# Attention of a two-model layer stack: heads in pairs on the two halves of TensorE's array, forget decays added by a selecting product

## What is computed

```
def causal_block_attention(q, k, v, log_forget_cum=None):
    s = einsum('bqhd,bkhd->bhqk', q_i, k) * dk ** -0.5
    if has_decay:
        s = s + d_queries[..., :, None] - d_keys[:, :, None, :]
    s = where(key_pos <= q_pos, s, -inf)
    p = softmax(s, axis=-1)
    return einsum('bhqk,bkhd->bqhd', p, v)

fox = causal_block_attention(fq, fk, fv, cumsum(log_sigmoid(f_logit + b_f), axis=1))
mla = causal_block_attention(q, k, v)
return concatenate([rms(fox), rms(mla)], -1) @ w_o
```

## Time and profile before

| | us |
|---|---|
| median of 3 runs | 2843.33 |
| lowest and highest of them | 2840.07, 2846.72 |
| the profiled execution | 2859.1 |
| its span | 2857.3 |
| TensorE busy | 2260.7 (79%) |
| VectorE busy | 687.8 (24%) |
| ScalarE busy | 372.7 (13%) |

### The profile page before, as it was taken

The page is one execution under the profiler, slowest core; times in us unless marked ns, Lnnn a source line. Parts: engine busy times, 40 slices in busy tenths (PEclk is TensorE's granted clock), DMA queues, the critical chain, the costliest instruction groups (busy, mean ns, idle before and its releaser), DMA issues. The chain is left out here.

```text
span 2857.3 us, 31837 instructions
## 1 busy us (share of the span) xinstructions
PE 2260.7 (79%) x13320; PEld 1411.6 (49%) x13321; DVE 687.8 (24%) x1524; ACT 372.7 (13%) x741; POOL 25.7 (1%) x28
## 2 busy tenths in 40 slices
PE   7897778899677996899866666689788998666765
PEld 5564436565244855778622222267576885222322
DVE  4352104352012135346300000012443112000001
ACT  1331001331001003110200000010312011000000
POOL 0000000000000000000000000000000000000000
PEclk9799899799898998889978888899988998878888
DMA  9138999135997340058499999964200345999997
GB/s 391 79 118 345 428 429 397 62 118 237 429 428 328 147 161 0 1 227 340 156 428 428 428 429 428 427 270 175 88 1 1 118 176 231 428 428 428 429 428 317
DMA packets 55834, 779.42 MB, mean 273 GB/s; under 512 B 6840, under 2 KB 7096, under 8 KB 8120
## 3 DMA queue, kind: packets, MB, share of 16 engines
q1 hardware_dynamic: 55736, 778.02, 65.5%
HBM read 776.95 MB, written 1.05 MB: 272 GB/s over the span
## 5 line engine op out<-in xcount | busy, mean ns | idle before, releaser
L1715 PE MATMUL bank<-ring,arena 128*32 128x512 f32 x3136 | 499.5, 773 | 337.7 <-DMA ring<-in_w_exp 334.2
L1715 PEld LDWEIGHTS bank<-ring,arena 128*32 128x32 f32 x3136 | 101.4, 126 | 728.4 <-DMA ring<-in_w_exp 494.3
L1740 PE MATMUL bank<-ring,arena 128*32 128x512 f32 x1568 | 197.4, 643 | 70.7 <-DMA ring<-in_w_exp 47.9
L853 PE MATMUL bank<-xnT,ring 128*128 128x256 f32 x960 | 212.7, 385 | 9.5 <-ACT xnT L368 9.5
L1895 DVE TENSOR_TENSOR arena<-bank,arena 128x256 f32<-128x256 f32 (+1 forms) x33 | 18.3, 554 | 787.6 <-PE bank L1715 559.3
L853 PEld LDWEIGHTS bank<-xnT,ring 128*128 128x128 f32 x960 | 185.6, 194 | 37.2 <-issue 11.2
L1446 PE MATMUL bank<-xnT,ring 128*128 128x256 f32 x768 | 178.5, 387 | 10.6 <-PEq L981 10.6
L1446 PEld LDWEIGHTS bank<-xnT,ring 128*128 128x128 f32 x768 | 149.1, 194 | 33.3 <-issue 12.2
L1685 PE MATMUL bank<-arena 128*128 128x256 f32 x592 | 141.5, 393 | 3.6 <-DVE arena L1906 3.6
L1685 PEld LDWEIGHTS bank<-arena 128*128 128x128 f32 x592 | 112.4, 195 | 62.8 <-issue 48.5
L1740 PEld LDWEIGHTS bank<-ring,arena 128*32 128x32 f32 x1568 | 50.7, 113 | 186.1 <-issue 95.6
(11 more groups left out here) (332 smaller groups left out, 2352.2 us busy)
## 6 DMA issues: line engine op xcount, KB each, us to landing
ring<-in_w_exp SPq DMA_DIRECT2D x288, 2048.0 KB, 25.7
arena<-in_w_ada SPq DMA_DIRECT2D x24, 2048.0 KB, 11.9
ring<-in_w_in SPq DMA_DIRECT2D x20, 2048.0 KB, 20.6
ring<-in_w_merge SPq DMA_DIRECT2D x18, 2048.0 KB, 8.5
ring<-in_w_o SPq DMA_DIRECT2D x8, 2048.0 KB, 11.2
ring<-in_w_conv SPq DMA_DIRECT2D x6, 2048.0 KB, 27.3
ring<-in_w_rest SPq DMA_DIRECT2D x2, 1696.0 KB, 25.7
small<-in_small SPq DMA_DIRECT2D x2, 1440.0 KB
```

The source lines that it names most:

```text
L853: last = nc.tensor.matmul(o[:, T * j:T * j + T], w[:, k, col:col + P], xnT[:, k, :], start=k == 0, stop=k == KT - 1)
L1715: last = nc.tensor.matmul(o[rows(e), :], Xw[:, k, rows(e)], ring[:, slot(n), at:at + MW], start=k == 0, stop=k == KT - 1)
L1740: last = nc.tensor.matmul(o[rows(e), :], hidT[:, j, rows(e)], ring[:, slot(n), at:at + MW], start=j == 0, stop=j == ft - 1)
```

## The change

The table of constants gets four columns `pair` in place of four columns `chunk`. Column j of `pair` is 1 on the partitions whose number within its half of 64 is j.

The heads are taken in the order 8 to 15, then 0 to 7, in eight pairs. Scores, transposes and value products are listed pair by pair (scores(i), turn(i-2), product(i-3) for pair i). Within a fox pair, the even head's products (partitions 0 to 63, one bank) and the odd head's (partitions 64 to 127, another bank) alternate; within every pair the two heads' value products alternate too.

The decays are formed once per layer. VectorE writes the scaled logs into a zeroed matrix `lfx` (two small operations), TensorE multiplies it with the triangle (two products), ScalarE copies the result to `decay` (128x256): the decays of the even fox heads on partitions 0 to 3, those of the odd on 64 to 67. A score bank gets its decay by a product of `pick` (64 rows that are zero except for one row of ones) with one half of `decay`, over 128 and 256 columns. GpSimd clears `lfx` and builds `pick`. Six buffers `zb` and four `pT` replace three and two. The scaling of the probabilities stays on VectorE, and so do the masks, the maxima, the reciprocals and the copies into `mixT`.

```
+    put("pair", p[:, None] % HD == np.arange(HEADS // 2)[None, :])
...
+            order = list(range(HEADS, NH)) + list(range(HEADS))
+            zb = [ar(3072 + 384 * i, COLS) for i in range(6)]
+            pT = [ar(5456 + 384 * i, COLS) for i in range(4)]
...
+                    def scores(i):
+                        if i >= 2:
+                            pe.wait_ge(z_ready, 2 * i - 2)
+                        pair = (2 * i, 2 * i + 1)
+                        if order[2 * i] >= HEADS:
...
+                            return
+                        pe.wait_ge(decay_ready, 1)
+                        pe.wait_ge(pick_ready, 1)
                         for t, (a, b) in enumerate(parts):
+                            for n in pair:
+                                h = order[n]
+                                nc.tensor.matmul(score_bank[n % 4][:, a:b], fqT[part(h), h // 2, P * t:P * t + P], fkT[part(h), h // 2, 0:b - a],
+                                                 start=t == 0, stop=False, skip_group_check=True)
+                        for t, (a, b) in enumerate(parts):
+                            for n in pair:
+                                h = order[n]
+                                last = nc.tensor.matmul(score_bank[n % 4][:, a:b], pick[part(h), h // 2, :], decay[part(h), 0:b - a],
+                                                        start=False, stop=t == 1, skip_group_check=True)
...
+                    def decays():
+                        pe.wait_ge(decay_in, 2)
+                        nc.tensor.matmul(bank[5][:, 0:T], lfx[:, 0, :], K("tri")[:, 0:T], start=True, stop=False)
+                        nc.tensor.matmul(bank[5][:, P:T], lfx[:, 1, :], K("tri")[:, T + P:2 * T], start=False, stop=True).then_inc(decay_made, 1)
...
+                    def turn(i):
+                        for n in (2 * i, 2 * i + 1):
+                            pe.wait_ge(p_ready, 2 * n + 2)
+                            if n >= 2:
+                                pe.wait_ge(pT_ready, n - 1)
...
+                    def product(i):
+                        pe.wait_ge(pT_ready, 2 * i + 2)
...
+                        for t in range(TT):
+                            for n in (2 * i, 2 * i + 1):
...
+                @block.gpsimd
+                def _(pool):
+                    nc.gpsimd.memset(lfx, 0.0).then_inc(decay_in, 1)
+                    nc.gpsimd.tensor_tensor(pick, K("ones").unsqueeze(1).broadcast_to([P, HEADS // 2, P]), K("pair").unsqueeze(2).broadcast_to([P, HEADS // 2, P]),
+                                            ALU.mult).then_inc(pick_ready, 1)
...
-                    def decays(h):
-                        if h >= 2:
-                            dve.wait_ge(scores_ready, h - 1)
                         for s in range(TT):
-                            last = nc.vector.tensor_scalar(Z[h % 2][:, s, :], K("tri")[:, T * s:T * s + T], lf[:, s, h:h + 1], -1.0 / scale[0],
-                                                           ALU.mult, ALU.mult)
+                            last = nc.vector.tensor_scalar(lfx[:, s, :].rearrange("p (o r) -> p o r", o=2)[:, :, 0:HEADS // 2], lf[:, s, :].rearrange("p (j o) -> p o j", o=2),
+                                                           -1.0 / scale[0], None, ALU.mult)
...
+                    for n in range(NH + 6):
+                        if n < NH:
+                            softmax(n)
+                        if n == 0:
+                            decays()
+                        if 1 <= n <= NH:
+                            finish(n - 1)
+                        if n % 2 == 1 and n >= 7:
+                            take((n - 7) // 2)
...
+                    nc.scalar.preload_act_table(ACT.Exp)
+                    for n in range(NH + 3):
+                        if n < NH:
+                            exps(n)
+                        if n == 1:
+                            act.wait_ge(decay_made, 1)
+                            nc.scalar.copy(decay, bank[5][:, 0:T]).then_inc(decay_ready, 1)
+                        if n >= 3:
+                            to_sbuf(n - 3)
```

More of the change, by code:

```diff
@@ L572, in attention @@
             NH = 2 * HEADS
+            NPAIR = NH // 2
             COLS = P + T
[L574 to L579, removed]
+            decay_in, decay_made, decay_ready, pick_ready, scores_ready, z_ready, top_ready, e_ready, r_ready, p_ready, p_turned, pT_ready, out_ready, out_taken = (
+                sem(f"att_{n}") for n in ("decayin", "decaymade", "decay", "pick", "scores", "z", "top", "e", "r", "p", "turned", "pT", "out", "taken"))
+            order = list(range(HEADS, NH)) + list(range(HEADS))
+            zb = [ar(3072 + 384 * i, COLS) for i in range(6)]
+            pT = [ar(5456 + 384 * i, COLS) for i in range(4)]
+            pick = ar(7000, HEADS // 2, P)
+            lfx = ar(7512, TT, P)
+            decay = ar(7768, T)
             score_bank = [bank[i] for i in (0, 1, 6, 7)]
@@ L614, in turn @@
-                    def turn(h):
-                        pe.wait_ge(p_ready, 2 * h + 2)
-                        if h >= 2:
[L617 to L628, removed]
@@ new lines, in decays @@
+                    def decays():
[7 more added lines that the diff above has]
+                                pe.wait_ge(pT_ready, n - 1)
+                            for k in range(3):
+                                last = nc.tensor.transpose(bank[2 + n % 2][:, P * k:P * k + P], zb[n % 6][:, P * k:P * k + P], K("ident"))
+                            last.then_inc(p_turned, 1)
@@ L672, in _, with softmax @@
-                    decays(0)
-                    decays(1)
-                    for i in range(NH + 3):
-                        if i < NH:
-                            softmax(i)
-                        if 1 <= i <= NH:
-                            finish(i - 1)
-                        if i + 2 < HEADS:
-                            decays(i + 2)
-                        if i >= 4 and i % 2 == 0:
-                            take((i - 4) // 2)
+                    def softmax(n):
+                        z = zb[n % 6]
+                        dve.wait_ge(scores_ready, n + 1)
+                        if n >= 6:
+                            dve.wait_ge(p_turned, n - 5)
+                        nc.vector.scalar_tensor_tensor(z, score_bank[n % 4][:, 0:COLS], scale[order[n] // HEADS], K("causal"), ALU.mult, ALU.add).then_inc(z_ready, 1)
+                        dve.wait_ge(z_ready, n + 1)
+                        for t, (a, b) in enumerate(parts):
+                            last = nc.vector.tensor_reduce(top[n % 2][:, t:t + 1], z[:, a:b], AX, ALU.max, negate=True)
+                        last.then_inc(top_ready, 1)
```

101 lines of the change are left out of this document (45 added, 56 removed).

## The result

| | before | after |
|---|---|---|
| median of 4 runs, us | 2845.02 | 2807.42 |
| lowest and highest | 2840.07, 2847.91 | 2802.06, 2810.78 |
| the profiled execution (span) | 2859.1 (2857.3) | 2802.06 (2800.1) |
| first attention stage | 60.2 | 35.4 |
| second attention stage | 57.1 | 34.8 |

The ratio is 0.9868, 95% interval [0.9846, 0.989]: 37.6 us faster, between 31 and 44. The forecast was a gain of 46.1 and 2797, with a range of 2785 to 2822. The time lies in the range. The two profiles differ by 57.0 us and the two medians by 37.6, and most of this document is about that difference. One of the 19 further timings of the old kernel that stand beside the first experiments, 3005.8 us at a granted clock of 0.784, was in a slower state and is in none of the ratios.

What follows compares the result with a forecast made beforehand. It took TensorE to bound the old fox heads and VectorE the mla heads; with VectorE setting the pace, stages of 35.6 us instead of 60.2 and 57.1 gain 46.1, so 2843.3 - 46.1 = 2797 us, range 2785 to 2822.

Steps and rivals of the forecast that it cites:

- What bounds the new stage: Attention at the full clock: VectorE sets the pace in all 16 heads, 3.94 us a pair against TensorE's 3.6.
- TensorE's terms: Fox pair on TensorE: scores with decays 1.8 us, transposes 2 x 0.47, value products 0.9, together 3.6 us.
- The price of 0.229 us: Fox scores and decays: a 256-column product from 64 rows costs 0.229 us, because the array's halves work at the same time.
- The opening and the decays formed once: Stage start: first masking at 0.1 + 0.96 us; two small VectorE operations 0.3 us, counted as nothing, bound 0.5 a layer.
- The sum of a stage: One attention layer: first masking, 15 steps of 1.77 us, five copies of 0.40, then 6.0 to the end: 35.6 us.
- The gain: Both attention stages: 24.6 and 21.5 us off the profiled 60.2 and 57.1, together 46.1, taken from the median 2843.3.
- unchanged in length: Sign of being right: outside attention, the rest of the program keeps its length.
- I take it that the level stays: TensorE's clock in attention stays at the full level, since mla scores begin right behind the barrier; forecast chance 0.63.
- The lower level at the opening: First rival: the clock falls as before, mla heads run slow, costing 11.8 and 9.2 us; 2818 us, chance 0.18.
- the second: Rival: TensorE's halves don't overlap; 5.5 us a fox pair, 4.3 an mla pair, 8 us a layer; 2813, chance 0.10.
- the third: Rival: each product waits for an empty array, clock low throughout; stage 85 us, 53 us slower, 2896; chance 0.03.
- `head_rms_out` gave nothing back: Sign of being wrong: this block now begins at the lower level and gives 2 to 3 us back a layer.

Runs made afterwards that it cites:

- new_with_Z4: New kernel with decays added the old way (two VectorE operations and three full products a fox head), in four buffers written four heads ahead; 2817.6 us, stages 39.5 and 38.0.
- new_again: The new kernel unchanged, for a second profile and more times; median 2809.57 us, ratio 0.9879 to the kernel before; stages 33.8 and 34.7 us.
- old_third: The kernel before, unchanged, for a third profile; 2842.05 us, stages 46.3 and 54.1 us.
- new_norm_pool: New kernel with the two scalings of the probabilities per head moved from VectorE to GpSimd; one execution, 2794.5 us, both stages 30.2 us.
- new_norm_pool_timed: The new kernel with the scalings on GpSimd, run again for timing; median 2803.2 us, ratio 0.9851 to the kernel before.
- new_held: New kernel with TensorE held back at the attention's opening by nine VectorE mask copies whose results are unused; 2823.6 us, stages 40.5 and 40.1.
- new_all_in_turn: New kernel with each pair's two heads one after the other in scores, decays and values, instead of alternating; 2821.3 us, stages 45.8 and 36.9.

## Why the prediction was right, and where it was off

**What bounds the new stage: right.** VectorE sets the pace at 1.77 and 2.10 us (forecast 1.77 and 2.17). Two runs confirm it by taking work away (copies to ScalarE, scalings to GpSimd) and one by adding some (new_with_Z4).

**TensorE's terms: right, somewhat high.** Fox scores of a pair took 1.51 us for 1.8, value products 0.80 for 0.9, transposes 0.81 for 0.94, together 3.12 for 3.6. The price of 0.229 us from the pattern of the earlier trace rows held. The full-overlap end was the true one for the value products.

**The opening and the decays formed once: right.** The first masking starts 0.97 us after the stage opens (forecast 1.06), both small operations take 0.23 us (0.3). GpSimd builds `pick` in 1.04 us (0.5 to 1.9), unseen on the path.

**The sum of a stage: right as a total.** The last masking starts 131.38 - 103.06 = 28.3 us in, not 29.6: four copies lie ahead of it, not five, and the first step is 1.27 us long because there is nothing to scale yet. The end takes 138.50 - 131.38 = 7.1 us, not 6.0, half of it at the lower level, and 6.5 in the second layer. The errors cancel: the stages are 35.4 and 34.8 us for 35.6.

**The gain: the term that was mis-sized.** The step was "60.2 - 35.6 = 24.6 and 57.1 - 35.6 = 21.5", carried over to the median. It holds between the two profiles (24.8 and 22.3). But 30.7 + 23.9 us at the lower level were far more than the 0 + 17.1 of later executions. Two more profiles of the same program, with totals at the median, have stages of 46.3 and 54.1 us: against new_again's 33.8 and 34.7 this is a gain of 31.9, not 46.1. The prediction saw the 15.8 us between profile and median, allowed "up to a few microseconds" for them, and counted none. As far as these profiles tell it was all of it: 117.3 - 100.4 = 16.9 us.

With the line above, the gain of 47.1 between the profiles splits. At the full level throughout, the old stages are 2 x 46.3 = 92.6 us. So 117.3 - 92.6 = 24.7 was the old kernel's time at the lower level, and 92.6 - 70.2 = 22.4 is what the new stages, with the low stretches that they have, gain on an old one without any. In old_third against new_again it is 7.8 and 92.6 - 68.5 = 24.1. That part is the fox heads': one took 3.44 us at the full level and takes 3.87 / 2 = 1.94 now, and 8 x 1.50 = 12.0 us a stage is 24 in both. The mla heads' step on VectorE is 1.77 us without a copy in both kernels. Inside the fox heads the decays have a price of their own (new_with_Z4); the larger number of buffers was never changed by itself, so what it gives is not shown.

**What made up for it.** 31.9 us in the stages is less than the 37.6 of the medians. In the profile pair old_third and new_again, 36.0 us apart in total, the second model's block gives 25.4 - 18.7 = 6.7 more. It was at 1.00 in both profiles of the new kernel and at 0.66 in all three of the old one, with equal work. The prediction had the rest of the program "unchanged in length". Whether the new kernel brings this about by shifting what follows in time, or whether five profiles fell so by chance, I didn't test; variants with other stage lengths had 22.3 to 27.5 us there. The code alone doesn't decide it: new_norm_pool and new_norm_pool_timed are one kernel, and that block took 25.4 and 27.5 us in their first layers and 19.4 and 25.1 in their second. That part of the measured gain is observed and not explained.

**"I take it that the level stays": half right.** It stayed at the opening in both profiles of the new kernel, and fell later once or twice for 3.4 us. It cost little because TensorE has 0.75 us of slack in a pair and is off the path. Where it falls matters: new_again has one low stretch of 3.4 us in each layer, in the middle of the first stage (from 117.8 us) and at the end of the second (from 541.0 us), where TensorE is on the path, and the second stage is 0.9 us longer. Through the one in the middle VectorE's maskings keep their distances (117.59, 119.36 and 121.46 us: 1.77 and 2.10).

**The rivals.** The lower level at the opening came in new_held as that rival had it, behind an idle TensorE, but at 1 to 2 us a layer and not 9 to 12. The halves do overlap, even when not alternated (new_all_in_turn), so the second and the third had no ground; the third's 3.3 us a head on TensorE was 1.56. `head_rms_out` gave nothing back.

## What to carry to other kernels

Before a gain is read off one profile, compare that profile's total with the median of the runs; where they differ, look for the stretch at the lower clock that makes the difference, and forecast from the stage at each level. Work on an engine that only waits is free to add and worth nothing to remove, until the bound moves to that engine; then each such operation counts at about its full length, as the decays did. Work moved to an idle engine can make that engine the next bound, as the scalings did with GpSimd. When a pair of engines is within a fifth of each other, slack on TensorE is worth having for its own sake, because its clock can halve.

## What the runs showed of the hardware

- One program had 0 or 30.7 us at the lower level in the same stage, and the stage was 46.3 or 60.2 us long, 0.455 us for each microsecond at the lower level. What decides it was not found. In all six stages of the three profiles TensorE was idle for the same 1.70 us before its first product; the level fell within 1.1 us of that product in four of them and stayed full in two.
- TensorE's clock can stay at the lower level for 30.7 us while the engine is busy in all of it: 106.3 to 137.0 us of the first profile and 119.2 to 149.9 us of new_all_in_turn.
- Products of two heads on different halves overlap without being interleaved: value products 0.80 us a pair either way, scores 2.27 in turn against 1.51 alternated, where two heads without overlap would need about 2.7 by the estimate in the prediction.
- GpSimd scales 128x128 elements in 0.60 us and 128x256 in 0.92, while VectorE's masking and its pair of maxima kept their 0.55 and 0.61 us beside it (new_norm_pool).
